# Fetching expert rows by indirect DMA in eight expert pairs instead of five, without the empty slots

## The reference

```
gates = top-8 of 64 sigmoid scores per token, normalised, times 2.5
hid   = silu(t @ exp_w1[e]) * (t @ exp_w3[e])          # D = 1024, D_EXPERT = 256
routed[t] = sum over e of (hid * gates[t, e]) @ exp_w2[e]
h = LN(alpha * h + routed + shared)
```

## Time and profile before

| what | value |
|---|---|
| median of three runs | 1493.3 us (1489.31 to 1493.69) |
| the profiled execution, its own time | 1490.3 us |
| its span, first to last instruction | 1488.5 us |
| granted TensorE clock over the span | 0.994 |
| PE busy | 1437.6 us, 97% |
| DVE, ACT, POOL busy | 724.7, 418.2, 205.4 us |
| DMA | 375.38 MB, mean 252 GB/s |

### The profile page before, as it was taken

One profiled execution on the slowest core, in us unless ns is written; L12 is line 12 of the kernel. 1 busy time (PEld: TensorE's weight loads), 2 busy tenths in 40 slices (PEclk: granted clock), 3 DMA queues, 4 the chain that ended last, 5 costly groups with the idle time before them and its releaser, 6 DMA issues.

```text
span 1488.5 us, 32593 instructions
## 1 busy us (share of the span) xinstructions
PE 1437.6 (97%) x13647; PEld 1051.5 (71%) x13647; DVE 724.7 (49%) x1345; ACT 418.2 (28%) x965; POOL 205.4 (14%) x171
## 2 busy tenths in 40 slices
PE   7999999999999999999999999999999999999995
PEld 6997666777776777777668986776575767676751
DVE  7445787875735777734547654522212121121228
ACT  2335434343223544435432211111111111111111
POOL 3771113122010000020022000000101000010000
PEclk9999999999999999999999999999999999999998
DMA  8888466363345444664576638599999999999984
GB/s 281 186 162 172 152 159 182 111 212 96 110 119 160 115 117 119 204 184 131 161 262 183 215 139 359 198 385 401 420 427 427 426 429 429 425 428 429 429 342 202
DMA packets 157042, 375.38 MB, mean 252 GB/s; under 512 B 101724, under 2 KB 110316, under 8 KB 139232
## 3 DMA queue, kind: packets, MB, share of 16 engines
q1 hardware_dynamic: 140928, 345.78, 65.8%
q0 software_dynamic: 6576, 16.48, 3.2%
q10 hardware_dynamic: 9392, 11.06, 2.2%
HBM read 327.14 MB, written 51.95 MB: 255 GB/s over the span
## 4 chain that ended last, share of the span: by engine, by line
PE 79%; DVE 9%; DMA 5%; DVEq 2%; issue 2%; ACT 1%; ACTq 1%; SPq 0%; POOLq 0%
PE PS L698 21%; PE PS L1250 14%; PE PS L1217 7%; PE PS L1269 6%; PE PS L1096 6%; PE PS L715 6%; DVE region L1730 4%; PE PS L780 3%; PE PS L1222 2%; PE PS L1138 2%; DVE region L1737 2%; DMA region<-projected 2%; PE PS L788 1%; PE PS L1233 1%; DMA region<-expert_rows 1%
## 5 line engine op out<-in xcount | busy, mean ns | idle before, releaser
L698 PE MATMUL PS<-h0T,region 128*128 128x320 f32 x1424 | 406.6, 438 | 1.0 <-issue 1.0
L1353 ACT ACTIVATE region<-PS 128x320 f32<-128x320 f32 (+7 forms) x408 | 154.5, 389 | 682.7 <-PE PS L698 233.1
L698 PEld LDWEIGHTS PS<-h0T,region 128*128 128x128 f32 x1424 | 264.0, 190 | 113.5 <-issue 12.1
L1250 PE MATMUL PS<-region 128*64 128x512 f32 x1024 | 228.8, 592 | 0.0
L1250 PEld LDWEIGHTS PS<-region 128*64 128x64 f32 x1024 | 124.4, 137 | 92.2 <-issue 32.0
L1730 DVE TENSOR_TENSOR region<-region 128x512 f32<-128x512 f32 (+10 forms) x230 | 154.3, 691 | 30.3 <-DMA region<-wo 6.5
L1353 ACT ACTIVATE region<-region 128x256 f32<-128x256 f32 (+11 forms) x229 | 99.4, 465 | 116.2 <-DVEq L2148 24.1
L1269 PE MATMUL PS<-region,history 128*64 128x512 f32 x512 | 119.7, 596 | 0.8 <-ACTq L1692 0.5
L1217 PEld LDWEIGHTS PS<-region,h 128*128 128x128 f32 x864 | 100.6, 192 | 22.3 <-issue 22.2
L1730 DVE TENSOR_TENSOR history<-region,PS 128x256 f32<-128x256 f32 x32 | 13.5, 421 | 196.5 <-ACTq L1687 196.4
L1217 PE MATMUL PS<-region,h 128*128 128x128 f32 x864 | 108.1, 278 | 0.3 <-issue 0.3
(11 more groups left out here) (239 smaller groups left out, 1594.8 us busy)
## 6 DMA issues: line engine op xcount, KB each, us to landing
region<-moe_w SPq DMA_DIRECT2D x64, 2048.0 KB, 17.9
region<-moe_w SPq DMA_DIRECT2D x64, 1024.0 KB, 15.6
region<-w_in SPq DMA_DIRECT2D x115, 512.0 KB, 5.7
region<-wo SPq DMA_DIRECT2D x32, 512.0 KB, 4.7
projected<-region ACTq DMA_DIRECT2D x64, 167.5 KB, 3.7
expert_rows<-region SPq DMA_DIRECT2D x20, 512.0 KB, 7.0
region<-expert_rows SPq DMA_DIRECT2D x5, 2048.0 KB, 15.2
region<-projected SPq DMA_DIRECT2D x10, 768.0 KB, 6.5
```

The lines of the kernel that those rows point to most:

```text
L698: last = mm(PS[:, 6 + i % 2, 0:NTOK], WR[:, i, k, :], H0T[:, k, :], start=(k == 0), stop=(k == KT - 1))
L1250: last = mm(PS[tiles(i), 2, :], XE[:, k, tiles(i)], W13[r][i][:, k * 512:k * 512 + 512], start=(k == 0), stop=(k == KT - 1))
L1353: return nc.scalar.activation(out, in_, f, **kw)
```

## The change

FETCHED becomes (8, 11, 14, 17, 20, 23, 26, 29). The token index of an empty slot becomes 4096 (SKIP), over the bound of 319, so that the fetch leaves it out as the scatter does; before it was 0, and row 0 was read for it. The table INFOF moves to another tile, since it has grown. The wait of the first projection tiles on their weights counts the 48 that the semaphore starts with.

```
-FETCHED = (6, 11, 16, 21, 26)
+FETCHED = (8, 11, 14, 17, 20, 23, 26, 29)
...
-        INFOF = shaped(HT[:, 2 * D + 384:2 * D + 474], 3, len(FETCHED), 2, 3)
+        INFOF = shaped(HF[:, 512:512 + 18 * len(FETCHED)], 3, len(FETCHED), 2, 3)
...
                 if ks[0] == 0:
-                    pe.wait_ge(sem(f"weights_in{i}"), (m + 1) * 16)
+                    pe.wait_ge(sem(f"weights_in{i}"), max((m + 1) * 16, 64))
...
                 ts(IDXF[:, k:k + 1], PS[:, 4, 5:6], float(SKIP), None, add)
-                ts(TOKF[:, k:k + 1], PS[:, 4, 6:7], 0.125, None, mul)
+                ts(TOKF[:, k:k + 1], PS[:, 4, 6:7], 0.125, float(SKIP), mul, add)
...
-                    dve.tensor_copy(INFOF[:, t, :, i, 2], VEC[:, V_TOK8 + t:V_TOK8 + t + 1].to_broadcast([128, len(FETCHED)]))
+                    ts(INFOF[:, t, :, i, 2], VEC[:, V_TOK8 + t:V_TOK8 + t + 1].to_broadcast([128, len(FETCHED)]),
+                       -8.0 * SKIP, None, add)
```

## The result

The change makes the kernel a little slower: 1495.75 us (median of 20 runs, 1491.61 to 1499.11) against 1491.19 us for the kernel before in the same comparison (20 runs, 1487.06 to 1493.69). The ratio is 1.0033, with a 95% interval of 1.0025 to 1.0041, so some 4.9 us of loss, 0.33%: at the edge of the 0.3% within which, by the prediction, a measurement tells nothing, and the interval takes that edge in. By this ratio the result lies just inside "slower by over 0.3%", which had a chance of 0.30, and not in the favoured class. The prediction named 1495.6 us, but from a base of 1493.3, as +2.3 us. That the time was met to 0.2 us is luck: the base was 2.1 us too high, and the step, 4.6 us by the medians and 4.9 by the ratio, was about twice the forecast.

What follows compares the result with a forecast made beforehand. The slowest DMA engine, busy with old work until 1441.3 us, was taken as the bound at the end, not PE. Terms +2.8 + 1.2 - 0.7 - 1.0 = +2.3 us took the median from 1493.3 to 1495.6 us, range 1490 to 1501.

Steps and rivals of the forecast that it cites:

- slower by over 0.3%: Outcome class for the whole kernel: measured slower than before by more than 0.3% (4.5 us); chance 0.30.
- the favoured class: Outcome class for the whole kernel: within 0.3% of the time before; chance 0.60.
- the 8.4 us that PE was to gain: PE to the end of pair 29: three more fetched pairs -11.2 us, three more infos +2.85 us; end not shortened.
- one sign of being wrong: Expert stage: the forecast is wrong if a pair takes longer than 16.17 us because DVE waits for a scatter.
- PE was the bound to the last: Rival, end of the kernel: the end follows scatter 29, -8.4 us with 3.4 given back, -5.0 us, 1488.3 us; chance 0.10.
- Three more fetched pairs, slowest engine: DMA after 1050 us: seven fetches put 49 rows on the slowest engine instead of 32, +2.8 us.
- Idle engines in the early part: Loads of pairs 8 to 10, issued up to 5.6 us later: between 0 and 2.8 us lost, taken as +1.2 us.
- The 0.95 us: PE's cost for each added `fetched_info`, where it waits for DVE's one-hot; three more, +2.85 us.
- PE's sum to the start of pair 29, -8.3 us: PE's running lateness through the stage: +5.6 us at pair 7, +2.8 from pair 8, -8.3 at pair 29.
- Absorbed: -1.7 us: Start of the row loads: 0.7 us since they were not yet moving, 1.0 us for an engine already late.
- the slowest engine gets no relief at all: Rival, landing of second row load: +4.0 us rows, +2.8 us idle early part, 0.7 absorbed: +6.1 us, 1499.4 us; chance 0.30.
- POOL and DVE: Fetches ahead of scatters: PE stalls every third pair covered by its 8 us lead if under some 2 us each; nothing.

Runs made afterwards that it cites:

- Run 3: The change with the filled slots spread over all DMA engines by a permuted slot row, nothing else; 1490.16 us, ratio 0.9998 to the kernel before.
- run 8: The change with every fetched slot's index over the bound, so its eight fetches transfer nothing; 1488.48 us, ratio 0.9986 to the kernel before.
- run 4: The kernel before with its slots spread over the DMA engines; 1489.5 us, ratio 0.9985 to the kernel before.
- 12: The change with spread slots and six fetched pairs (6, 10, ..., 26), pair 31's step in its old place; 1490.75 us, ratio 0.998 to the kernel before.
- run 1: The change with eight fetches, but empty slots read row 0 again; 1497.2 us, ratio 1.0037 to the kernel before.
- run 7: The change with its eight fetched pairs at 6, 9, ..., 27; 1493.4 us, ratio 1.0024 to the kernel before.
- run 9: The change with spread slots, fetched pairs 6 to 27, pair 31's step between first and second sum; 1489.39 us, ratio 0.9973 to the kernel before.
- run 5: The change with pair 31's hidden step on DVE moved ahead of the first two sums; 1493.84 us, ratio 1.0024 to the kernel before.

## Why the prediction was right or wrong

**Right: what sets the end.** PE was busy for 97% of the span before and the chain ran through it, and yet the 8.4 us that PE was to gain came to nothing; the slowest of 16 DMA engines decides when the rows can be summed. Run 3 (spreading alone, -5.2 us), run 8 (no fetched rows, -7.0 us) and the constant 4.8 to 4.9 us from the last old landing to the first rows show it. These signs named in advance held: q0 with 9.42 MB where 9.21 were before, the engines fading later and the vectors landing later, the first DVE sum late and the end of the chain going through DMA into the sums.

Other signs failed. Pair 29 was 5.0 us earlier and not 7 to 8. Its scatter landed at 1441.15 us, where 1434.4 was forecast (its own terms add up to 1434.6): it went out late, behind the chain of scatters, and not with PE. And one sign of being wrong came true: two pairs took longer than 16.17 us, 16.7 each, because DVE waited for a scatter. Here is PE in the first of them (its `hidden` starts at 1318.57, the next at 1335.27), and its last bracket names the step of DVE behind the eviction:

```profile
1322.62 3.65 PE L1250 MATMUL PS<-region 128*64 128x512 f32 x16 [0.45 <-DVEq L2453]
```

That cost 1 us of PE's time in all and nothing at the end.

The rival "PE was the bound to the last" is excluded for the change itself; it is what the kernels become once their slots are spread (runs 4 and 12).

**Wrong: the sum, +2.3 where +4.9 was measured (+5.8 in the profiled execution).** Step by step:

- *Three more fetched pairs, slowest engine: +2.8 us, bounds +0.6 and +4.0.* Run 8 gives 6.9 rows for the slowest engine where 7 were taken, run 1 gives 7.7, less surely. So the term stands between (7 x 6.9 - 32) x 0.165 = +2.7 and, with 7.7, +3.6. Leaving out empty slots takes 3.8 us from the mean engine and 0.4 to 0.6 us, both within the noise, from the end: the rule of the Trainium skill, page "DMA: Bandwidth & Descriptors", section "The descriptor swizzle", which stood beside the sum at its upper bound of +4.0, was near the mark.
- *Idle engines in the early part: +1.2 us, bounds 0 and 2.8.* This is the step that failed: the term was taken at less than half its size. The argument was "nearer to 0 since a fetch of 128 rows goes away just there". Of the vectors' 6.4 us, 2.7 to 3.6 us are rows, which leaves 2.8 to 3.7 us for this one; pair 14's weights are 2.9 us late already. The bytes show 5.0 us lost before 1120 us. That is a mean over the engines, and the mean landing is indeed 5.3 us later with 0.6 us of more rows; that the slowest engine, which has the most work and so is idle least, lost less than the mean is my reading. Run 7 seems to take 2.6 us of it back by fetching from pair 6, but run 9 doesn't repeat it. That a fetch goes away there was no help; a likely reason, not tested alone, is that it shortens a queue where there was hardly one yet.
- *Why PE was later in that part than forecast.* Pairs 6 and 7 together take 1094.85 - 1063.17 = 31.7 us in the chain after, where 16.52 for pair 6 and 12.43 + 0.95 for pair 7, 29.9, were forecast. The rows:

```profile
1063.17 6.92 PE PS L1250 x31
...
1081.03 9.40 DMA expert_rows<-region,row_index
1090.57 0.69 DVE region L2449
...
1093.46 0.69 DVEq L2435
1094.19 0.54 PE PS L1289 x10
1094.85 6.92 PE PS L1250 x31
```

  `fetched_info` (L1289) needs DVE's one-hot (L2435), and DVE's eviction of the next rows (L2449), ahead of it, waits for scatter 6 to land. A pair of 12.43 us is too short to hide a landing of 9.4 us and the info's one-hots. The 0.95 us came from a pair of 16.17 us, and I had used it for a short one.
- *PE's sum to the start of pair 29, -8.3 us.* Measured -5.0: pair 29 starts at 1409.50 where 1413.22 was the start before, less the 1.3 us of the stage's own start. Besides the 1.8 us above, two evictions held PE by 0.5 us each late in the stage; some 0.5 us stays open. The lateness up to pair 8 counts in the term above; the rest doesn't matter for the end.
- *Absorbed: -1.7 us.* Between the vectors (+6.4) and the second sum (+4.1) 2.3 us went, so this was about right.
- *Not in the sum: +1.7 us for pair 31.* With rows this late, DVE's order holds PE's last pair, and the fourth sum waits for it. The trace of run 5 shows just this gone (5.84 us in place of 7.50 from the third sum to the fourth). I had followed the chain to the second sum and taken for granted that the rest would shift as a block.

The rival "the slowest engine gets no relief at all" had +6.1 us from +4.0 for rows, +2.8 for the early part and -0.7: the measured terms lie nearer to it than to mine, and the result, +4.9 us, nearer to it too. It should have had the larger chance.

**Wrong, without weight for the end:** POOL and DVE. I expected stalls around scatters to be covered, and put the scatters' own chain at nothing. DVE's idle time for POOL in the stage grew from 71.5 us in 13 waits to 131.2 us in 19:

```profile
DVE region L2449 <- POOLq L2734: 131.2, 19, 10.6
```

PE noticed 1 us of it late in the stage, but 1.8 us at pair 7, where it cost DMA time. With 15.2 us for a scatter against 14.9 for a pair, POOL and DVE would be the next bound of a version with still more fetched pairs; no run tests that.

## What to carry to other kernels

A mean DMA share at its limit hides which engine is last: look at how the engines fade at the end of a full stretch, and if they fade over many microseconds, spread the filled slots over the partitions before trading work between engines (here it was worth 5.2 us to one kernel and 2.2 us to the other, at no cost that the runs show). When a stretch is bound by a queue of transfers, work taken from the computing engine later doesn't help, and lateness in the part where the queue is still empty can come out at the end nearly whole (some 3 us here); compare bytes moved there, not shares. A chain in the profile isn't yet the bound: when it goes through scatters, look whether what follows starts as soon as they land or a fixed time after something else. And follow the chain to its very end: an order of steps on VectorE that is free at one landing time costs some 2 to 3 us at another, in either direction.

## What the runs showed of the hardware

- An indirect transfer with rows left out loads the 16 DMA engines by partition, not evenly. Leaving out 371 rows took 0.6 us from the time, give or take 2, and rearranging the rows on the partitions 5.2 us, with the same bytes; the 16 parts of the vectors' landing moved from 10.0 to 3.2 us apart.
- A short stall of PE costs more than itself. In run 1 pair 29 waits for its weights:

```profile
1410.40 8.78 PE L1250 MATMUL PS<-region 128*64 128x512 f32 x32 [2.87 <-DMA region<-moe_w]
```

  and in the windows around it the granted clock (the third number from the right) falls:

```profile
1405.00:1410.00 5.00, 2.53 (x12) 0.57 (x8) 2.37 (x9) 0.69 (x1) 0.00 (x0) 1.00 1.01 429
1410.00:1415.00 5.00, 4.60 (x14) 1.77 (x16) 0.20 (x1) 0.00 (x0) 0.97 (x1) 0.66 1.03 437
```

  0.66 in a stretch is part of it at the lower of the two levels, 1.2 GHz, after PE had been busy for 2.53 of 5 us. The 32 matmuls take 8.78 us, where a `hidden` at the full clock takes 6.9: a wait of 2.9 us cost 1.9 us more. Run 1 shows how thin the lead over the weights has become with eight fetches; in the change pair 29's weights land at 1372.2 + 36.6 = 1408.8, 0.7 us before PE takes them up at 1409.50.
- The start of the expert stage varies by 6.5 us between profiled executions (957.1 in run 7, 963.6 in run 4) of kernels whose edits lie behind that point, constants aside; that is more than the change's own effect.
